# First norm's modulation in eight groups by feature chunk, with its first two panels' products between them

## What is computed

```python
m = silu(c) @ ada_w + ada_b                  # 9 parts of 1024, one set for latents, one for context
h = rms_norm(x, norm1_w) * (1 + m[1]) + m[0]
x = x + 0.5 * m[2] * ((silu(h @ ffn1_w1) * (h @ ffn1_w3)) @ ffn1_w2)
```

## Time and profile before

| | us |
|---|---|
| median of 3 runs | 2047.36 |
| the three runs | 2048.18, 2045.96, 2047.36 |
| span of the profiled execution | 2046.2 |
| its own total | not given apart from the span |
| TensorE busy | 1951.9 (95%) |
| VectorE busy | 1019.1 (50%) |
| ScalarE busy | 834.6 (41%) |
| GpSimd busy | 835.9 (41%) |

### The profile page before, as it was taken

One profiled execution on the slowest core, in us unless ns is written; L12 is line 12 of the kernel. 1 busy time (PEld: TensorE's weight loads), 2 busy tenths in 40 slices (PEclk: granted clock), 3 DMA queues, 4 the chain that ended last, 5 costly groups with the idle time before them and its releaser, 6 DMA issues.

```text
span 2046.2 us, 25933 instructions
## 1 busy us (share of the span) xinstructions
PE 1951.9 (95%) x9514; PEld 1643.3 (80%) x9514; DVE 1019.1 (50%) x1527; ACT 834.6 (41%) x1276; POOL 835.9 (41%) x414
## 2 busy tenths in 40 slices
PE   4999999999989999889999999999899989999998
PEld 2999999999978875567888888877667767888886
DVE  3869877657457215965213112578964352121124
ACT  4525252434355135562532233446665444232231
POOL 1337574656424221442443443533612224353432
PEclk8999999999989999789999999999999999999999
DMA  8133342433312220002232232332311212232321
GB/s 351 52 134 129 130 175 103 163 131 119 114 62 72 72 71 31 11 22 88 84 112 92 94 108 86 111 115 83 102 43 52 72 52 85 90 113 82 113 82 62
DMA packets 53487, 197.68 MB, mean 97 GB/s; under 512 B 6320, under 2 KB 7056, under 8 KB 51600
## 3 DMA queue, kind: packets, MB, share of 16 engines
q1 hardware_dynamic: 52240, 191.47, 26.8%
q10 hardware_dynamic: 1152, 4.92, 0.7%
HBM read 194.27 MB, written 2.10 MB: 96 GB/s over the span
## 4 chain that ended last, share of the span: by engine, by line
PE 81%; DVE 10%; issue 4%; ACT 4%; DMA 1%; SPq 0%; POOL 0%; DVEq 0%; ACTq 0%
PE ps L2301 44%; PE ps L2430 13%; PE ps L2467 8%; PE ps L2315 2%; PE ps L2288 1%; PE ps L2289 1%; PE ps L2290 1%; PE ps L2832 1%; PE ps L2656 1%; PE ps L2647 1%; PE ps L2728 1%; PE ps L2850 1%; DVE ada_prod L1425 1%; DVE rg_t L2201 1%; DVE s_gla L1990 1%
## 5 line engine op out<-in xcount | busy, mean ns | idle before, releaser
L655 POOL TENSOR_TENSOR wlo<-raw,whi 128x1024 fp32r<-128x1024 f32 x244 | 601.5, 2475 | 988.7 <-ACT whi L708 964.4
L708 ACT ACTIVATE whi<-raw 128x1024 fp32r<-128x1024 f32 x244 | 253.6, 1053 | 270.1 <-PE ps L2301 187.9
L2301 PE MATMUL ps<-h_hi,whi 128*128 128x512 f32 (+1 forms) x960 | 353.3, 383 | 2.8 <-DVE act_a L1582 1.7
L2301 PE MATMUL ps<-h_hi,wlo 128*128 128x512 f32 (+1 forms) x960 | 351.0, 380 | 0.0
L2301 PE MATMUL ps<-h_lo,whi 128*128 128x512 f32 (+1 forms) x960 | 350.5, 380 | 0.0
L662 POOL TENSOR_TENSOR wlo<-raw,whi 128x512 fp32r<-128x512 f32 x108 | 161.1, 1506 | 134.1 <-ACT whi L876 133.7
L2301 PEld LDWEIGHTS ps<-h_hi,whi 128*128 128x128 f32 x960 | 176.7, 188 | 40.1 <-issue 5.4
L2301 PEld LDWEIGHTS ps<-h_lo,whi 128*128 128x128 f32 x960 | 176.3, 188 | 33.3 <-issue 1.0
L2301 PEld LDWEIGHTS ps<-h_hi,wlo 128*128 128x128 f32 x960 | 176.5, 188 | 32.8
L2301 PE MATMUL ps<-g_hi,whi 128*128 128x512 f32 x432 | 168.3, 390 | 0.0
L2301 PE MATMUL ps<-g_lo,whi 128*128 128x512 f32 x432 | 168.3, 389 | 0.0
(11 more groups left out here) (482 smaller groups left out, 3730.0 us busy)
## 6 DMA issues: line engine op xcount, KB each, us to landing
raw<-panels SPq DMA_DIRECT2D x280, 512.0 KB, 3.3
ada_w<-ada_t SPq DMA_DIRECT2D x56, 512.0 KB, 3.9
ada_f<-ada_p SPq DMA_DIRECT2D x8, 1024.0 KB, 17.1
x_lat<-x_t SPq DMA_DIRECT2D x1, 2048.0 KB, 7.9
out<-x_lat SPq DMA_DIRECT2D x8, 256.0 KB, 2.2
x_ctx<-ctx_t SPq DMA_DIRECT2D x1, 1024.0 KB, 9.9
cond_b<-cond SPq DMA_DIRECT2D x1, 1024.0 KB, 21.8
x_ctx<-mem_t ACTq DMA_DIRECT2D x1, 1024.0 KB, 4.8
```

The source lines that it names most:

```text
L655: pool.tensor_tensor(wlo[:, sl], raw[:, sl], whi[:, sl].bitcast(f32), ALU.subtract).then_inc(lo_done, 1)
L708: act.activation(whi[:, sl], raw[:, sl], ACT.Copy).then_inc(hi_done, 1)
L2301: ins = pe.matmul(bank(banks + b, n), wt[:, w], a[:, at_(kc, c0):at_(kc, c0) + n], start=kc == 0 and j == 0, stop=kc == n_k - 1 and j == 2)
```

## The change

- `ada_p` is laid out anew on the host: group k now holds, for all 1024 input rows, the 128 shift and the 128 scale columns of feature chunk k. It is 1 MB as before, and each group alone completes the modulation of one chunk.
- SP's loads: x in two halves, group 0 and 1, panels 0 and 1, groups 2 to 7, panels 2 and 3, then the condition for later parts and the small loads that are used much later. ScalarE issues the four small loads that are needed at once. It also loads its function tables ahead (`preload_act_table_set`).
- TensorE makes the rows of group k (`modulation_rows`: 8 products of 256 columns in four quarters), ScalarE copies them, and TensorE sums the quarters and turns them into columns at once (`modulation_columns`: 2 products with the selector `row_sel`). VectorE's `modulation(k)` makes bias and scale of chunk k just before it scales chunk k.
- `head` sets TensorE's order: rows, columns and the first two panels' products of the chunks alternate. `first_pair` is no longer called here. Panels 2 and 3 are rounded after all chunks.

```diff
-ADA_COLS = ADA_PE * P
+ADA_COLS = 2 * P
...
         def _(sp):
-            sp.dma_start(x_lat[:, :], x_t).then_inc(x_loaded, 16)
-            sp.dma_start(x_ctx[:, :], ctx_t).then_inc(x_loaded, 16)
-            sp.dma_start(vec[:, :], vecs).then_inc(vec_loaded, 16)
-            sp.dma_start(cond_s[:, :], cond_t).then_inc(condt_loaded, 16)
-            sp.dma_start(lsig[:, 0:8], decays.partition_broadcast(P)).then_inc(small_loaded, 16)
+            for e in range(2):
+                h = slice(e * KC // 2 * LAT, (e + 1) * KC // 2 * LAT)
+                sp.dma_start(x_lat[:, h], x_t[:, h]).then_inc(x_loaded[e], 16)
+                h = slice(e * KC // 2 * CTX, (e + 1) * KC // 2 * CTX)
+                sp.dma_start(x_ctx[:, h], ctx_t[:, h]).then_inc(x_loaded[e], 16)
+            for k in range(KC):
+                sp.dma_start(ada_f[k][:, :], ada_p[k]).then_inc(ada_loaded[k], 16)
+                if k == 1:
+                    for s in range(2):
+                        sp.dma_start(raw[:, s * PANEL:(s + 1) * PANEL], panels[s]).then_inc(raw_ready[s], 16)
...
                 if m.n == 0:
+                    modulation_row(0)
+                    modulation_row(1)
                     round_panel(0, 1)
                     round_panel(1, 1)
-                    act.wait_ge(ada_rows_done, 1)
-                    act.activation(ada_row[:, :], bank(5), ACT.Copy).then_inc(ada_copied, 1)
...
-                    if m.n == 0 and kc in (3, 4):
-                        round_panel(kc - 1, 1)
+                    if m.n == 0 and kc + 2 < KC:
+                        modulation_row(kc + 2)
+                if m.n == 0:
+                    round_panel(2, 1)
+                    round_panel(3, 1)
...
+            def modulation_row(k):
+                act.wait_ge(ada_rows_done, k + 1)
+                act.activation(ada_row[k % 2][:, :], bank(4, ADA_COLS, k % 2 * ADA_COLS), ACT.Copy).then_inc(ada_copied, 1)
...
+            act.dma_start(cond_s[:, :], cond_t).then_inc(condt_loaded, 16)
+            act.dma_start(vec[:, :], vecs).then_inc(vec_loaded, 16)
+            act.dma_start(lsig[:, 0:8], decays.partition_broadcast(P)).then_inc(first_loaded, 16)
+            act.dma_start(ident[:, :], ident_h).then_inc(first_loaded, 16)
+            act.preload_act_table_set("exp_and_others")
             act.wait_ge(vec_loaded, 16)
-            act.wait_ge(small_loaded, 96)
+            act.wait_ge(first_loaded, 32)
...
+            act.preload_act_table_set("sqrt_and_others")
...
+            def modulation(k):
...
+                dve.wait_ge(ada_mods, k + 1)
+                dve.tensor_tensor(both[:, :, k:k + KC + 1:KC], bank(5, 4, 4 * k).rearrange("p (q r) -> p r q", r=2), bias, ALU.add)\
+                    .then_inc(mods_ready, 1)
+                dve.wait_ge(mods_ready, k + 1)
+                link(dve.scalar_tensor_tensor(scales[:, 0:2 * KC].rearrange("p (j c) -> p j c", j=2)[:, :, k], both[:, :, KC + k], 1.0,
+                                              vcol("norm1_w", k).broadcast_to([P, 2]), ALU.add, ALU.mult))
...
+            def modulation_rows(k):
+                pe.wait_ge(ada_loaded[k], 16)
+                for kc in range(KC):
+                    j = kc % 4
+                    ins = pe.matmul(ps[32 * j:32 * j + 32, 4 * 512 + k % 2 * ADA_COLS:4 * 512 + (k % 2 + 1) * ADA_COLS], cond_w[:, kc * 32:(kc + 1) * 32],
+                                    ada_f[k][:, kc * ADA_COLS:(kc + 1) * ADA_COLS], start=kc < 4, stop=kc >= 4)
+                ins.then_inc(ada_rows_done, 1)
+            def modulation_columns(k):
+                pe.wait_ge(ada_copied, k + 1)
+                if k:
+                    pe.wait_ge(mods_ready, k)
+                for q in range(2):
+                    ins = pe.matmul(bank(5, 2, 4 * k + 2 * q), ada_row[k % 2][:, q * P:(q + 1) * P], row_sel, start=True, stop=True)
+                ins.then_inc(ada_mods, 1)
+            def head():
+                pe.wait_ge(consts, 4)
                 pe.wait_ge(condt_ready, 1)
+                modulation_rows(0)
+                norm_means(norms[0])
+                pe.wait_ge(first_loaded, 32)
+                norm_spread(norms[0])
+                pe.wait_ge(sel_ready, 1)
+                modulation_columns(0)
+                modulation_rows(1)
+                modulation_columns(1)
+                for kc in range(KC):
+                    if kc + 2 < KC:
+                        modulation_rows(kc + 2)
+                    for c in range(2):
+                        if kc == 0:
+                            pe.wait_ge(lo_done, c + 1)
+                        pe.wait_ge(h_ready, kc + 1)
...
+                        if c == 0 and kc + 2 < KC:
+                            modulation_columns(kc + 2)
...
             pe.sem_inc(panel_done, RING)
-            first_modulation(0, KC // 2)
-            norm(norms[0])
-            first_modulation(KC // 2, KC)
+            head()
             first_layer()
```

More of the change, by code:

```diff
@@ L563, in _ @@
         def _(sp):
-            sp.dma_start(x_lat[:, :], x_t).then_inc(x_loaded, 16)
-            sp.dma_start(x_ctx[:, :], ctx_t).then_inc(x_loaded, 16)
-            sp.dma_start(vec[:, :], vecs).then_inc(vec_loaded, 16)
-            sp.dma_start(cond_s[:, :], cond_t).then_inc(condt_loaded, 16)
-            sp.dma_start(lsig[:, 0:8], decays.partition_broadcast(P)).then_inc(small_loaded, 16)
+            for e in range(2):
[8 more added lines that the diff above has]
+                        sp.dma_start(raw[:, s * PANEL:(s + 1) * PANEL], panels[s]).then_inc(raw_ready[s], 16)
+            for s in range(2, RING):
+                sp.dma_start(raw[:, s * PANEL:(s + 1) * PANEL], panels[s]).then_inc(raw_ready[s], 16)
+            sp.dma_start(cond_b[:, :], cond.partition_broadcast(P)).then_inc(cond_loaded, 16)
             sp.dma_start(lr_raw[:, :], lr_w).then_inc(small_loaded, 16)
@@ L1518, in norm @@
                         b = (kc % 2) * TOK
+                        if m.n == 0:
+                            modulation(kc)
                         if m.n == 0 and kc >= 2:
@@ L2222, in _ @@
             dve.wait_ge(vec_loaded, 16)
-            dve.wait_ge(small_loaded, 96)
+            dve.wait_ge(first_loaded, 32)
+            dve.tensor_reduce(out=row_sel, in_=ident[:, :].rearrange("p (j c) -> p c j", c=32)[:, 0:2, :], axis=AX.X, op=ALU.add)\
+                .then_inc(sel_ready, 1)
             log_sigmoids()
@@ L2228, in _ @@
             token_factors(norms[0])
-            dve.wait_ge(ada_mods, 1)
-            for r in range(2):
-                c = r * NMOD * KC
-                src = bank(4).rearrange("p (q j x) -> p j q x", q=4, j=ADA_TILES)[:, :, :, r]
-                link(dve.tensor_tensor(mods[:, c:c + ADA_PE].rearrange("p (j q) -> p j q", q=4), src,
-                                       vcol("ada_b", 0, ADA_PE).rearrange("p (j q) -> p j q", q=4), ALU.add))
-            norm_scale(0, 0, 1, "norm1_w")
-            norm_scale(1, 1, 1, "norm1_w")
             norm(norms[0])
@@ L2382, in norm @@
                 ins.then_inc(rstd_ready, 1)
-            def first_modulation(k0, k1):
-                pe.wait_ge(condt_ready, 1)
-                for kc in range(k0, k1):
-                    pe.wait_ge(ada_loaded[kc], 16)
-                    for j in range(ADA_TILES):
-                        ins = pe.matmul(ps[32 * j:32 * j + 32, 5 * 512:6 * 512], cond_w[:, kc * 32:(kc + 1) * 32],
-                                        ada_f[kc][:, j * 512:(j + 1) * 512], start=kc == 0, stop=kc == KC - 1)
-                if k1 == KC:
-                    ins.then_inc(ada_rows_done, 1)
-                    pe.wait_ge(ada_copied, 1)
-                    for q in range(4):
-                        ins = pe.transpose(bank(4, P, q * P), ada_row[:, q * P:(q + 1) * P], ident[:, :])
-                    ins.then_inc(ada_mods, 1)
+            def norm(m):
+                norm_means(m)
+                norm_spread(m)
@@ new lines, in head @@
+            def head():
+                pe.wait_ge(consts, 4)
+                pe.wait_ge(condt_ready, 1)
+                modulation_rows(0)
[13 more added lines that the diff above has]
+                        pe.wait_ge(h_ready, kc + 1)
+                        w = slice(c * PANEL + kc * P, c * PANEL + (kc + 1) * P)
+                        for j, (wt, a) in enumerate(((whi, h_hi), (whi, h_lo), (wlo, h_hi))):
+                            for b, c0, n in halves(TOK):
+                                ins = pe.matmul(bank(2 * c + b, n), wt[:, w], a[:, hidden_at(kc, c0):hidden_at(kc, c0) + n],
+                                                start=kc == 0 and j == 0, stop=kc == KC - 1 and j == 2)
+                        if kc == KC - 1:
+                            ins.then_inc(panel_done, 1)
+                        if c == 0 and kc + 2 < KC:
+                            modulation_columns(kc + 2)
```

47 lines of the change are left out of this document (20 added, 27 removed).

## The result

| | before | changed |
|---|---|---|
| median, us | 2047.19 (4 runs, 2045.96 to 2048.18) | 2056.97 (4 runs, 2055.92 to 2058.01) |
| span of the profiled execution | 2046.2 | 2054.8 (its own time 2056.68) |
| end of the last low part | 62.33 | 70.90 |

The account below looks back on a forecast made before the run. TensorE holds 81% of the chain, so only its idle start could change. Start, prologue and turns summed to a last low part at 63.7 against 62.33; +1.4 on 2047.36 gave 2048.8 us, range 2041 to 2055.

Parts of the forecast that it names:

- start: First ScalarE operation, once its four small loads land: at 8.5 us, the middle of bounds 4.6 and 12.5.
- start to end of additions: From the first small operation to the end of the squares' last addition: stays 13.0 us, ending at 21.5.
- means, root, spread: Means, root and the transposes that spread 1/rms, after the additions: 5.0 us, to 26.5.
- spread to end of low part 0: Prologue: columns, rows, copy, roundings, high part, low part and 0.4 of contention, from 26.5 to 34.1 us.
- six turns: Chunk loop: a first turn of 5.8 us at 1.2 GHz plus five of 4.5, 28.3 in all, to 62.4.
- last low part: End of the chunk loop: waits only for its high part, adds 1.3 us, ends at 63.7 against 62.33.
- small loads wait for x: Rival at the start: small loads land only with x, start at 12.5, +4.0 us, time 2052.8; chance 0.10.
- Contention: Prologue: GpSimd's subtractions for panels 0 and 1 slow VectorE's first low part by 0 to 2.6 us, taken as 0.4.
- The loop: Chunk turns: low part, product, columns, scales, chunk, next low part wait on each other, 4.5 us a turn where 2.45 before.
- The clock rival: Turns: TensorE's idle of about 1.1 us each drops the clock, three cold turns give +5.1 us, 2053.9; chance 0.14.
- So +1.4: Stall after the first layer, 131.5 to 135.08: absorbs TensorE's 2.0 us delay and passes on VectorE's 1.4.
- The loads put at nothing: Group loads during the chunks: hidden, costing only if 12 us late; no TensorE wait for a group's load after group 1.

Follow-up runs that it names:

- e2: Changed kernel with its four small loads issued by SP ahead of x instead of by ScalarE beside x; 2049.19 us.
- e4: Changed kernel, small loads still on ScalarE's queue but ordered vectors, decays, condition, identity, first operations waiting for the first two only; 2052.05 us.
- e3: Changed kernel with panels 0 and 1 rounded by ScalarE before the root of the means; 2053.29 us.
- e12: Changed kernel with added constant products in TensorE's idle time (92, 70, 4 and 30 at four places before the first chunk's product); 2068.51 us.
- e6: Changed kernel with the columns of group k+2 made behind both products of chunk k instead of behind the first; 2066.15 us.
- e8: Changed kernel with columns of group k+2 ahead of both products of chunk k and rows of group k+3 between them; 2052.53 us.
- e13: e9 with 54, 6 and 2 added constant products on TensorE and the root between the two roundings; 2042.35 us.
- e7: Kernel before the change, with condition, vectors, decays and identity loaded ahead of x on SP and later-used small loads put last; 2044.21 us.
- e9: Changed kernel with the edits of e2, e3 and e8 together; 2042.99 us.

## Why the prediction was wrong

Step by step, forecast against the changed kernel's trace:

| step | forecast | measured | off by |
|---|---|---|---|
| start | 8.5 | 13.4 | +4.9 |
| start to end of additions | 13.0 | 12.9 | -0.1 |
| means, root, spread | 5.0 | 4.95 | 0 |
| spread to end of low part 0 | 7.6 | 9.4 | +1.8 |
| six turns | 28.3 | 28.9 | +0.6 |
| last low part | 1.3 | 1.3 | 0 |

- **The step that failed is the start.** I bounded the landing by "at worst all wait for x: 12.5" and took the middle of the two bounds, for want of a row. The measured 13.4 lies beyond the worse one, because the two queues moved packet for packet: the fourth small load came with x's last part and 0.5 behind it, and x itself was in only at 12.8, not at the 11.1 on which the bound was built. e2 and e4 show it: e4's condition, third in line, takes 9.0 us for 8 KB, and ahead of x the four take 1.8 to 2.5. The rival "small loads wait for x" was the right mechanism. It had 0.10, and its price of +4.0 was 0.9 too low.
- The Trainium skill (DMA: Bandwidth & Descriptors, Queues, rings and completion order) was weighed there, with its rule of turns packet by packet and an estimate of 7.1 for the start. The trace agrees with the rule, 603 packets of one queue beside 573 of the other, and not with the estimate. The estimate put 32 packets of x an engine at 4.8 us, 0.15 each; in the changed kernel's transfer records they took 0.35 (8192 bytes) and 0.21 (4096), together 8.9. With 8.9 in place of 4.8 the same estimate gives a start of 11.2.
- **Contention was mis-sized.** "It costs 0 to 2.6, and I take 0.4, since the first subtraction is nearly over by then": the first was nearly over, as forecast (35.24 to 37.6, the low part from 37.14 on), but the second followed at 37.57, and no term stood for it. The low part's second operation took 2.57 beside it. In all the contention measured 2.35; the upper bound, from the row of the same pair of engines, was the better value. e3 took it away.
- **The loop was right**, in place and size: 4.43 for 4.5 a turn, the wait for the columns 1.81, the first turn 5.75 for 5.8. That the second turn was slow too (5.47) is the 0.6; e12 shows that it is the clock. e6 (longer by one product) and e8 (open) confirm the loop from both sides. One part of it was sized too low: TensorE's own work in a turn was put at 3.4, and in e8, where it waits for nothing, a turn takes 3.73.
- **The clock rival was wrong for this kernel**, granted 1.00 from 47.4 on with TensorE waiting 0.60 us in each turn; in e6, with 1.75, it came true. The rule of the Trainium skill (TensorE: Matmul & The Clock Gate, A second HAM failure mode: psum-queue depth-cycling), by which short idles make the clock swing, holds in e6 and not in the changed kernel.
- **The path behind the first layer was not as put.** The prediction let the stall take up TensorE's shift and pass on VectorE's ("So +1.4"). Between these two kernels TensorE's 9.15 arrived at the stall, 0.6 more than the 8.57 of the last low part; at the end of the span the difference is 8.6. No run was made for this. In e6 TensorE's step to panel 2 comes 9.1 later than in the changed kernel, the last low part 7.6 and the stall's end 8.3, between the two, so what rules there stays open. The stall itself stayed, 3.59 for 3.58.
- The loads put at nothing were nothing: no wait of TensorE for a group after the first rows.

The errors lie on one path and add: 4.9 + 1.8 + 0.6 - 0.1 = 7.2, and 63.7 + 7.2 = 70.9. A start at the worse bound (+4.0) and the full contention (+2.2) would together have given 2055.0, just the upper end. The time lies above it because the start was 0.9 later than its bound and the second turn ran at 1.2 GHz.

## What to carry to other kernels

Loads that everything waits for go on the same queue ahead of the bulk, not on a second queue beside it, where they passed at one packet for each packet of the bulk. An order that interleaves a small dependent product with large ones must put a whole product between the small one and each engine that it goes through; moving it to the front alone only moves the wait. And when a path has been shortened at its head, ask first what a simple repair of the old plan would give: here moving the small loads ahead gave the old kernel 3.4 us, and the new plan, with all its repairs, about 2 more at most (e13 against e7, whose intervals overlap).

## What was not expected of the hardware

- A load of 4 to 100 KB on ScalarE's queue beside SP's four large ones landed 0.2 to 0.5 us behind the load of the same place on SP's queue (5.3, 7.3, 9.2 and 11.2 after 5.1, 6.9, 9.0 and 10.7), while ahead of them on SP's own queue it took 1.8 to 2.5.
- Some operations on VectorE were held through most of a GpSimd subtraction even when tiny, and others were not. Held: `scales<-mods,vec`, 2.28 instead of 0.16 us (e13), and the pair `h_lo<-prod,mods,h_hi`, 3.50 instead of 1.14 (changed kernel). Not held: `mods<-ps,vec` with 0.17 at 23.98 in e13, and `prod<-x_lat,scales,ps` with 0.75 at 35.31 in the changed kernel, both beside a subtraction. The latter read an operand from TensorE's output `ps`, the former do not.
- The clock column says nothing of the first stretch. The trace has no clock record before the level first changes (to 1.00, at 33.7 in the changed kernel and 36.7 in e9), and the windows print 1.00 where they have no record. In e9, 16 passes took 1.93 at 24.37 and 1.07 at 38.57, with 1.00 printed for both. Before the first record only the durations tell the pace; from there on the two agree.
